# Six stages that follow each other without a full stop, and the delta rule's gates as 64x64 tiles

## The reference, cut to what matters

```python
# layer 0: attention over a window of 128, gated
proj = h @ w_in + b_in                       # q, k, v, z
x = x + rmsnorm((o * silu(z)) @ w_out + b_out, post_norm_w[0])
# layer 1: gated recurrence, 8 heads of 128 x 128
x = x + rmsnorm((o * silu(z)) @ w_out, post_norm_w[1])
# layer 2: one half gated linear attention, one half delta rule
log_a = log_sigmoid(glr @ gla_gate_up + gla_gate_bias) / 16
o_inter = einsum('nbhid,nbhdv->nbhiv', q_in, S_prev)   # chunks of 64 tokens, state 64 x 128
w = -softplus(-(rwkv_w0 + tanh(wl) @ rwkv_w_up)) - 0.5 # gates: 64 -> 512
a = sigmoid(rwkv_a0 + al @ rwkv_a_up)                  # gates: 64 -> 512
S = S * w_t + sa * (kk_t * a_t) + v_t * k_t            # 8 heads, state 64 x 64
x = x + concat(gla_out, rwkv_out) @ w_out
```

## Time and profile before

| what | us |
|---|---|
| median of 3 runs | 3875.42 (3875.19 to 3876.66) |
| the profiled execution, its own time | 3874.09 |
| its span, first to last instruction | 3872.8 |
| PE busy | 3606.7 (93%) |
| DVE, ACT, POOL busy | 2010.7, 1657.5, 1163.7 |
| mean granted TensorE clock | 0.969 of full speed |

### The profile page before, as it was taken

One profiled execution on the slowest core, in us unless ns is written; L12 is line 12 of the kernel. 1 busy time (PEld: TensorE's weight loads), 2 busy tenths in 40 slices (PEclk: granted clock), 3 DMA queues, 4 the chain that ended last, 5 costly groups with the idle time before them and its releaser, 6 DMA issues.

```text
span 3872.8 us, 78702 instructions
## 1 busy us (share of the span) xinstructions
PE 3606.7 (93%) x32928; PEld 2762.4 (71%) x32928; DVE 2010.7 (52%) x4568; ACT 1657.5 (43%) x3040; POOL 1163.7 (30%) x1406
## 2 busy tenths in 40 slices
PE   7999979999799999999998969999999997899999
PEld 4555547778688787878776857777777775787777
DVE  4655553255555556555555445666666655334322
ACT  2444442132455556555554334344443442344432
POOL 0000001032354545454543323222222220444332
PEclk9999999999899999999998989999999998899999
DMA  3000000032201010101002331111111112322132
GB/s 124 29 1 1 1 12 17 17 131 87 67 23 44 23 45 23 45 23 45 23 23 98 131 128 40 40 40 40 37 38 35 45 35 89 87 71 72 48 127 87
DMA packets 220223, 202.66 MB, mean 52 GB/s; under 512 B 7072, under 2 KB 191840, under 8 KB 219872
## 3 DMA queue, kind: packets, MB, share of 16 engines
q1 hardware_dynamic: 219872, 197.62, 16.3%
HBM read 164.04 MB, written 33.55 MB: 51 GB/s over the span
## 4 chain that ended last, share of the span: by engine, by line
PE 76%; DVE 8%; ACT 7%; POOL 4%; issue 3%; DMA 2%; SPq 0%; DVEq 0%; ACTq 0%; POOLq 0%
PE bank L194 17%; PE bank L196 16%; PE bank L195 16%; PE bank L448 5%; ACT arena L188 3%; PE bank L2296 2%; DVE arena L686 2%; PE bank L1172 2%; PE bank L2307 2%; ACT L278 1%; POOL arena_cut L1935 1%; PE bank L488 1%; ACT arena L189 1%; ACT arena_cut L188 1%; PE bank L312 1%
## 5 line engine op out<-in xcount | busy, mean ns | idle before, releaser
L195 PE MATMUL bank<-hT_cut,arena_cut 128*128 128x512 f32 x2080 | 823.1, 396 | 0.0
L188 ACT ACTIVATE arena<-bank 128x512 f32<-128x512 f32 (+1 forms) x584 | 314.6, 569 | 535.4 <-PE bank L196 305.0
L194 PE MATMUL bank<-hT_cut,arena_cut 128*128 128x512 f32 x1112 | 502.3, 452 | 0.0
L188 ACT ACTIVATE arena<-arena 128x512 f32<-128x512 f32 (+3 forms) x690 | 353.5, 549 | 261.4 <-POOL arena L1361 191.9
L195 PEld LDWEIGHTS bank<-hT_cut,arena_cut 128*128 128x128 f32 x2080 | 397.2, 191 | 83.2 <-issue 18.3
L196 PE MATMUL bank<-hT_cut,arena_cut 128*128 128x512 f32 x1112 | 440.3, 396 | 0.0
L189 ACT ACTIVATE arena<-arena 128x256 f32<-128x256 f32 (+2 forms) x336 | 210.2, 627 | 503.9 <-DVE arena L178 276.5
L194 PE MATMUL bank<-arena_cut,hT_cut 128*128 128x512 f32 (+1 forms) x960 | 365.9, 381 | 42.8 <-DVE arena_cut L1006 33.2
L2565 POOL TENSOR_TENSOR arena_cut<-arena,arena_cut 128x256 fp32r<-128x256 f32 x272 | 223.8, 852 | 475.2 <-ACT arena_cut L188 475.2
L195 PE MATMUL bank<-arena_cut,hT_cut 128*128 128x512 f32 (+1 forms) x960 | 360.9, 376 | 0.0
L194 PE MATMUL bank<-oT_cut,arena_cut 128*128 128x512 f32 x712 | 311.1, 437 | 33.9 <-POOL arena_cut L2565 23.1
(11 more groups left out here) (237 smaller groups left out, 7071.6 us busy)
## 6 DMA issues: line engine op xcount, KB each, us to landing
arena<-in_w_in SPq DMA_DIRECT2D x100, 512.0 KB, 3.8
arena<-in_rec_w_in SPq DMA_DIRECT2D x64, 512.0 KB, 4.1
x_after<-arena SPq DMA_DIRECT2D x32, 512.0 KB, 2.6
arena<-x_after SPq DMA_DIRECT2D x32, 512.0 KB, 4.2
oT<-in_x SPq DMA_DIRECT2D x16, 512.0 KB, 3.4
arena<-in_x SPq DMA_DIRECT2D x16, 512.0 KB, 3.4
h_after<-hT SPq DMA_DIRECT2D x4, 2048.0 KB, 7.7
hT<-h_after SPq DMA_DIRECT2D x4, 2048.0 KB, 17.2
```

Of the source, the lines that this page charges most:

```text
L188: return e.activation(out, a, f, bias=bias, scale=scale)
L194: pe.matmul(out, a[0], b[0], start=start, stop=False)
L195: pe.matmul(out, a[0], b[1], start=False, stop=False)
```

## The change

- **Stages.** `phase` only notes what the stage before counted; each engine calls `settle` for itself, at a place of its own. Before it, SP waits for those products alone (`freed`) that read the weights' old place, and loads the first weights of the next stage; ScalarE rounds and POOL subtracts them, each behind its last instruction of the stage before. Gate: two blocks. Recurrence: four. Delta rule and gated linear attention: one, and the wide one. Output stages: one, four and five of the eight chunks of w_out; these are subtracted by POOL in four pieces each, the others by VectorE as before. In the first tile of an output stage PE goes through the chunks once, six products each, for both halves. For this `wq` moves to the front of the attention's arena and `wide` to that of gated linear attention, and the two arrays of an output stage's weights are interleaved.
- **Gate stage.** h's group g+1 is rounded and subtracted ahead of unit g, and POOL's subtraction is in four pieces.
- **Delta rule.** The gates are 16 products of 64x64x128, and a0 takes a bank of `cb`. Rounding and subtraction of the next group stand in the last z block; PE counts each of z's steps for that. The first unit's front has 25 ticks.
- **Gated linear attention.** The wide weights are rounded in q and subtracted in two halves, in q and z0; the state's products are 64x64x64; the back of every second unit is a tick longer.

```diff
     def phase(self):
 
-        for e in (self.pe, self.act, self.dve, self.pool, self.sp):
-            for s in self.every:
-                if s.n:
-                    e.wait_ge(*s.end())
+        self.before = [s.end() for s in self.every if s.n]
         self.every, self.used, self.table = [], 0, None
+
+    def settle(self, *engines):
+
+        for e in engines:
+            for s in self.before:
+                e.wait_ge(*s)
 
...
     def in_turn(columns, cut, unit):
-        columns(0)
         for f in range(KC):
             for g in range(NG):
-                if f == 0:
-                    cut(g)
-                if g == 1 and f + 1 < KC:
+                if f == 0 and g == 0:
+                    cut(0)
+                if f == 0 and g + 1 < NG:
+                    cut(g + 1)
+                if g == 1 and 0 < f < KC - 1:
                     columns(f + 1)
...
+        for done in freed:
+            sp.wait_ge(*done)
+        columns(0)
+        columns(1)
+        k.settle(sp)
         in_turn(columns, nothing, nothing)
...
             pool.wait_ge(*w_a.by("hi", f))
-            pool.tensor_tensor(w_lo[f % 2], raw[f % 2], w_hi[f % 2], ALU.subtract).then_inc(*w_p.did("lo"))
-
+            for c in range(0, KC, 2):
+                ins = pool.tensor_tensor(w_lo[f % 2][:, c:c + 2, :], raw[f % 2][:, c:c + 2, :], w_hi[f % 2][:, c:c + 2, :], ALU.subtract)
+            ins.then_inc(*w_p.did("lo"))
+
+        columns(0)
+        columns(1)
+        k.settle(pool)
...
+    k.freed = [(0, z_pe.by("z", (KC - 1) * NG - 1))]
...
-        for c in range(KC):
+        for c in early + later:
+            if c in freed:
+                sp.wait_ge(*freed[c])
+            elif c == later[0]:
+                k.settle(sp)
             sp.dma_start(wo[:, c, :], w_out[c * P:(c + 1) * P, :]).then_inc(*w_got[c].did("in"))
...
+            pe.wait_ge(*c_p.by("lo", t))
+            if t == 0:
+                pair = [banks.take(f"m{n}", t)[0] for n in range(2)]
+                for c in order:
+                    pe.wait_ge(*(w_p.by("lo", early.index(c)) if c in freed else w_v.by("lo", later.index(c))))
+                    for n in range(2):
+                        ins = piece(t, c, n, pair[n])
+                        if c == order[-1]:
+                            ins.then_inc(*m_pe.did(f"m{n}"))
+                return
...
+        for c in early:
+            rounded(c)
+        k.settle(a)
         cut(0)
         cut(1)
-        for c in range(KC):
-            a.wait_ge(*w_got[c].by("in"))
-            act(a, wo_hi[:, c, :], wo[:, c, :], ACT.Copy).then_inc(*w_a.did("hi"))
+        for c in later:
+            rounded(c)
...
+        for n, c in enumerate(early):
+            pool.wait_ge(*w_a.by("hi", n))
+            for i in range(4):
+                part_of = slice(256 * i, 256 * i + 256)
+                ins = pool.tensor_tensor(wo_lo[:, c, part_of], wo[:, c, part_of], wo_hi[:, c, part_of], ALU.subtract)
+            ins.then_inc(*w_p.did("lo"))
+        k.settle(pool)
         cut(0)
         cut(1)
         in_turn(cut, nothing, rest)
...
+    k.freed = [m_pe.end()]
...
+        for i, _ in pieces:
+            split(i, 0)
+        k.settle(a)
         for c in range(KC):
             round_h(0, c)
...
+    k.freed = [(i, Fpe.by(name, UN - 1)) for i, name in pieces]
...
+        for done in freed:
+            sp.wait_ge(*done)
         load_v(0)
+        load(0)
+        k.settle(sp)
         sp.wait_ge(*cleared.by("wg"))
         sp.dma_start(wg[:, :, 0:16], k.columns_of(w_in, GLA_R, 16)).then_inc(*g_got.did("in"))
         sp.wait_ge(*cleared.by("up"))
         for r in range(4):
             sp.dma_start(up[32 * r:32 * r + 16, :], k.ins["gla_gate_up_2"][0]).then_inc(*u_got[r].did("in"))
-        load(0)
         sp.dma_start(k.tables["gla"], k.ins["table"][:, o:o + G]).then_inc(*t_got.did("in"))
         sp.dma_start(n_at[0][:, 0:P], k.ins["table"][:, o + G:o + w]).then_inc(*m_got.did("in"))
...
-                        if n == 0 and j == 0 and u == 0:
-                            pe.wait_ge(*wv_p.by(f"lo{c}"))
+                        if n == 0 and j == 0:
+                            pe.wait_ge(*wv_p.by(f"lo{c}", u))
...
             for i in range(8):
                 t0 = slice(i * CH, (i + 1) * CH)
                 for h in range(2):
-                    ins = pe.matmul(outs[h][:, t0], s3[half(h), i, :], q_at[u % 2][half(h), t0], start=False, stop=(i == 7))
+                    for m in range(2):
+                        ins = pe.matmul(outs[h][half(m), t0], s3[half(h), i, half(m)], q_at[u % 2][half(h), t0], start=False, stop=(i == 7))
             ins.then_inc(*Bpe.did("o"))
...
-            yield from block("q", u)
+            yield from block("q", u, {2: lambda: wide_split(u + 1)})
...
-            yield from block("q", u)
+            yield from block("q", u, range(4))
 
         def gates(u):
-            yield from block("z0", u)
-            for c in range(KC):
-                if c == 0:
-                    split(index("z1", u) + 1)
-                if c == 2:
-                    wide_split(u + 1)
-                yield
-
+            yield from block("z0", u, range(4, KC))
+            yield from block("z1", u)
+
+        wide_split(0, range(KC))
+        split(0)
+        k.settle(pool)
         pool.memset(wg, 0.0).then_inc(*cleared.did("wg"))
         pool.memset(up, 0.0).then_inc(*cleared.did("up"))
         for h in range(2):
             pool.memset(sc_at[h], 0.0).then_inc(*cleared.did(f"sc{h}"))
-        wide_split(0)
-        split(0)
         in_turn(nothing, front, gates, nothing)
...
+    k.freed = [(c, Fpe.by("v1", UN - 1)) for c in range(2)] + [
+        (2 + (BN - 4 + i) % 3, Fpe.by(kinds[i], UN - 1)) for i in (1, 2, 3)]
...
-    def in_turn(solve, scores, carry, front):
+    def in_turn(cut, solve, scores, carry, front):
 
         rounds = 10
+        run(cut(0))
         for i in range(SN + 4):
             stream = lambda f, back: f(i - back) if 0 <= i - back < SN else iter(())
             late = [stream(solve, 3), stream(scores, 2), stream(carry, 4)]
-            ahead, ticks, went = stream(front, 0), 17 + (16 if i % 8 == 0 else 0), 0
+            ahead, ticks, went = stream(front, 0), 17 + (8 if i % 8 == 0 else 0), 0
             for n in range(rounds):
...
                 if p == 0:
                     pe.wait_ge(*g_a.by("tanh", g))
-                for r, name in enumerate(("w0", "a0")):
-                    if u == 0:
+                if u == 0:
+                    for r in range(2):
                         pe.wait_ge(*up_got[r].by("in"))
-                    b = bank(fb, name, u)
-                    mm(b, up[half(r), p * P:(p + 1) * P], wa[half(r), :], start=True, stop=True).then_inc(*Fpe.did(name))
+                b = [bank(fb, "w0", u), bank(cb, "a0", u)]
+                for n in range(4):
+                    t0 = slice(n * P, (n + 1) * P)
+                    for r, name in enumerate(("w0", "a0")):
+                        for m in range(2):
+                            ins = mm(b[r][half(m), t0], up[half(r), p * P + m * CH:p * P + (m + 1) * CH], wa[half(r), t0], start=True, stop=True)
+                        if n == 3:
+                            ins.then_inc(*Fpe.did(name))
 
...
+        def round_h(g, c):
+            if g in (1, 2):
+                a.wait_ge(*Fpe.by("z" if c == KC - 1 else f"z_{c}", 4 * g - 1))
+            act(a, hi_of(g, c), k.hT[:, c, cols_of(g)], ACT.Copy).then_inc(*h_a.did("hi"))
+
+        def cut(g):
+            for c in range(KC):
+                round_h(g, c)
                 yield
 
...
-                yield from block("z", g, p)
+                turn = p == 3 and g + 1 < NG
+                yield from block("z", g, p, {c: (lambda c=c: round_h(g + 1, c)) for c in range(KC)} if turn else {})
...
+        def rest_h(g, c):
+            v.wait_ge(*h_a.by("hi", g * KC + c))
+            v.tensor_tensor(lo_of(g, c), k.hT[:, c, cols_of(g)], hi_of(g, c), ALU.subtract).then_inc(*h_v.did("lo"))
+
+        def cut(g):
+            for c in range(KC):
+                rest_h(g, c)
+                yield
+
+        def block(mid={}, turn=None):
             for c in range(KC):
                 if c in mid:
                     mid[c]()
+                if turn is not None:
+                    rest_h(turn, c)
                 yield
```

131 lines of the change are left out of this document (77 added, 54 removed).

## The result

The changed kernel takes 3809.14 us in the median of four runs (3808.36 to 3811.12), against 3875.31 before: 66.2 us less, a ratio of 0.9829 with an interval of 0.9812 to 0.9846. The sign was right and the size was not: 3783 was forecast, and the measured time lies 3 us outside the range of 3760 to 3806. The profiled execution has a span of 3809.8 us for 3872.8, 63.0 less. One run of this study, of experiment 8, took 7952 us in a slow state and is left out.

The account below looks back on a forecast made before the run. PE, busy 93% of the time, was taken to bound the kernel. The terms summed to 92.7, about 92 us, off 3874.1, giving 3782 and, with 1.3 for the median, 3783 us; range 3760 to 3806.

Parts of the forecast that it names:

- the attention gate's stage: Attention to gate: weights prepared ahead and cut(g+1) ahead of unit g start the fourth unit's last product sooner, 19 us.
- two tiles at a time: Rival, chance 0.06: gates need 1.9 us, not 1.0, and the mixer's state products gain nothing; 3804 us.
- The mixer: Gated linear attention: state products 7.7 us, wide weights 11, start -1.
- The start: Into the gated mixer: small weight's DMA waits for clearing after 12 POOL pieces, but wide weights are ready; -1 us.
- the state products: Gated mixer: 32 products of 64x64x64 take about 1.05 us instead of 2.00, in eight units; 7.7 us.
- the wide weights: Gated mixer: split pieces done a block earlier remove PE's seven waits on POOL and one low-clock stretch; 11 us.
- Into the recurrence: Start of the recurrence: weights come while the last tile is normed, PE starts near 991.2, not 999.03; 8 us.
- Second and third output stage: A loss: POOL's 16 and 20 pieces precede cut(0), ending first tiles 4.6 and 8.1 us later; -13.
- The gates and the clock behind them: Delta rule: 64x64 gates save 1.9 us in 16 units, 31 us; four half-speed stretches behind them go, 7.
- some 0.8 us stay: Delta rule, four units that open a group: r block's wait for k's bank behind the gates, 0.8 us.
- The turns: Delta rule, three group changes: moving next group's rounding and subtraction into the last z block gives 4 us each, 12.
- Into the delta rule: Start of the delta rule: weights land at 2279.6, rounding and four pieces end at 2283.8, not 2290.70; 7 us.

Follow-up runs that it names:

- experiment 8: Changed kernel, at the start of the recurrence ScalarE rounds one weight, then h, then the other three weights: 3803.9 us in three runs.
- Experiments 7: Changed kernel, SP issues the recurrence's and delta rule's first weight loads ahead of the last tile's stores: 3799.2 us.
- experiment 5: Changed kernel, in the second and third output stage the vector engine starts its own chunks only after POOL has cut tile 0: 3799.3 us.
- experiment 4: Changed kernel, in the output stages the vector engine subtracts all eight weight chunks and POOL only cuts tiles: 3783.0 us.
- experiment 1: Kernel before the change with only the 64x64 gates, a0 in a bank of the carry's ring: 3841.8 us, ratio 0.9921.
- Experiment 3: Changed kernel with both gate products in banks of the carry's ring: 3796.5 us.
- experiment 2: Changed kernel, delta rule turns as before: rounding and subtraction of the next group's h in eight ticks of their own: 3816.5 us.

## Why the prediction was right in sign and too large

Right, by its own steps: the gates' 32 passes in about 1 us (0.92); a plain unit at 55 us; no wait between the gates and none for the carry's update in any unit; the attention gate's stage (19, 16.3); and the sign of the second and third output stage. The 32 passes of a unit's gates end within 1.10 us; two tiles at a time, they would have taken 1.9 by the prediction's estimate. The condition that was cited there for overlap (TensorE: Matmul & The Clock Gate, Part 3, in the Trainium skill) does not limit this order of tiles, by the measured 0.92.

The mixer came out near its forecast (17.7, 18.6) by misses that cancel, which is luck. The start lost 4.7 us where 1 was booked; the state products gave 5.6 to 6.7 for 7.7; the rest, booked at 11 for the wide weights, is about 17. By the windows of the stage PE is idle 9.5 us less in it (the 10.0 of the wide pieces are gone, and waits for h go from 3.4 to 4.8), and its work falls by 13.7, of which 7 are not the state products but the clock, where one low stretch was booked. No experiment took it apart.

The clock gave more than its term in the delta rule too: PE's work falls there by 28.2 us, of which the gates' passes explain 18.2, so that an estimated 10 are clock where 7 were booked. It hides part of what the waits fell short by.

Wrong:

- *Into the recurrence, 8 for 0.6.* The step "the weights now come while the last tile is normed" failed. The loads are free to start, but they stand behind the last store of x on SP's queue, and land when h is complete; then four roundings stand ahead of h on ScalarE. Experiments 7 and 8 show it: with the loads ahead, PE's wait is 2.69 us, and the forecast's was 2.9. (The start alone came 1.6 us sooner; the stage behind it took 1.0 us of that back.) The same queue was seen at the delta rule (the loads "stand behind that store") and not here.
- *Second and third output stage, -12.7 for -19.7.* The step "16 pieces, 11.0" took a piece at its median. Beside a vector-engine subtraction of 128x1024 with two inputs it takes 1.7 us (experiment 5 took the vector engine away and had 11.36 us for the sixteen; experiment 4 took the pieces away). The sixteen pieces took 4.3 us more than booked and the twenty of the third stage 3.4 more, which is the miss of 7. The same group of rows held the warning: a longest piece of 1580 ns, a longest tile of 3386 for 2340. The Trainium skill has it as a rule (SBUF — State Buffer, "SBUF: two separate sides"): a vector operation with two inputs in SBUF and a GpSimd operation that reads SBUF lock each other out for a whole instruction. The runs agree: 1.71 and 1.74 us beside each other, 0.72 and 1.22 alone, so that each takes nearly the sum of the two.
- *The gates and the clock behind them, 38: by experiment 1 31.6 in the medians, 36.4 in the delta rule of its trace.* Nothing was wrong in the plain units. The passes' term took 1.9 us sixteen times, though the prediction itself said that 0.8 of it stay in the four units that open a group; they gave 1.1, and 0.4 to 0.6 at the turns: 26.3 for 31. At the turns the step "some 0.8 us stay" failed: 2.1 stay with the gates alone and 3.07 in the changed kernel, since k's bank is freed by ScalarE and the vector engine only after a table change and the end of the carry. Experiment 3 took the wait away and found 12.7 us behind it, the waits themselves and the low clock that follows them, less the new waits of 1.24.
- *The turns, 12 for 7.4.* Half of what the turns lose was taken, for want of a row; experiment 2 puts it at 7.4, with 9.3 and 6.5 as the other readings.
- *Into the delta rule, 7 for 3.6.* The chain of weight, rounding and four pieces was right to 1.0 us (its last piece ends at 2274.3, 14.1 us after the last product before, for 13.1). It overlooked that the table's load now goes out behind the weights, and that the vector engine waits for it ahead of h's first subtraction.

The terms of the starts and turns erred on the same side, since most of them were read as "the old wait goes", with the next wait put at its shortest. Taken together with signs the misses are 30 us. The range counted them as if they varied apart.
